# Joining the attention branches in two whole-width steps, with a new schedule table, in a one-core transformer block

## Chip, cores and metric

One NeuronCore of one Trainium2 chip runs the whole kernel in a single launch. The metric is the device time of one execution in microseconds (us); the program has the five engines TensorE (PE), VectorE (DVE), ScalarE (ACT), GpSimd (POOL) and SyncE (SP), each with its own instruction stream, and hand-placed semaphores between them.

## What is computed

One layer of a transformer over 1024 tokens of width 1024, in float32. The attention part has three families of four or eight heads of width 64: NSA (three branches, joined by a gate), sliding window with sinks (SWA) and stick-breaking (SB). The lines that matter for this change are those of the NSA family:

```python
def nsa_mixer(q, k_cmp, v_cmp, k_slc, v_slc, k_win, v_win, gate_logits, ...):
    ...
    o_cmp, o_slc = nsa_cmp_and_select(q, kc, vc, k_slc, v_slc, bias_tab)
    o_win = banded_attention(q[:, None], k_win[:, None], v_win[:, None], NSA_WINDOW, bias_tab)
    g = jax.nn.sigmoid(gate_logits.astype(jnp.float32)).reshape(b, s, 3, h).transpose(2, 0, 3, 1)[..., None]
    return g[0] * o_cmp + g[1] * o_slc + g[2] * o_win
...
    return jnp.concatenate([rms_norm(merge_heads(o_nsa), grp_g[:w_a]), rms_norm(merge_heads(o_swa), ...), rms_norm(merge_heads(o_sb), ...)], axis=-1)
...
        x = x + rms_norm(mix @ w_out[l], ln_attn_post[l])
        h = rms_norm(x, ln_ffn_pre[l])
        f = (jax.nn.silu(h @ ffn_w_gate[l]) * (h @ ffn_w_up[l])) @ ffn_w_down[l]
        x = x + rms_norm(f, ln_ffn_post[l])
```

## The kernel before

The time falls into three stages. Up to about 120 us the projections of the input are made. From there to about 505 us the attention runs. After that come the output projection and the feed-forward part, to the end at 1236 us.

The attention works in **jobs**. A job is one kind of attention (`sb`, `swa`, `win`, `cmp`, `slc`) for one tile of 128 query rows and four heads. There are 8 `sb`, 16 `swa` and 24 NSA jobs; the NSA ones come last, for each row tile in the order `win`, `cmp`, `slc`. Each job goes through the same steps. `query_hi`/`query_lo` split the queries (ACT L1269, DVE L1449), and four DMAs, `spread` on the SP queue (L812), place them for PE. `scores` on PE (L1070, L1078) multiplies queries and keys into one of four PSUM banks. `logits` on DVE (L1480) adds the bias and takes the running minimum `m_neg`; it frees the PSUM bank for the next `scores`. `softmax` on ACT (L1275) exponentiates. `turn` on PE (L1105) transposes the weights, `keep` copies them to SBUF (ACT L1305 or DVE L1510), and `weigh` on PE (L1125) multiplies them with the values into PSUM bank 7, the only bank for sums.

`combine` on DVE takes the sums out of bank 7. It first makes the four coefficients (L1533 or L1530, then a reciprocal, L1536). For `swa` and `win` one tensor_tensor of 128x256 multiplies all four heads with the coefficients, broadcast over the head width, into the tile `mix` (L1540). For `cmp` and `slc`, whose result is added to what is in `mix`, four scalar_tensor_tensor instructions of 128x64 do it, one for each head (L1546). The first `weigh` of the next job waits for the last instruction of the previous job's `combine`, as there is one bank of sums. After `slc`, `squares` on ACT (L1325), `mean_squares` on DVE (L1552), `root` on POOL (L894) and `norm_mix` on DVE (L1560) normalize `mix`, and PE transposes it (L1094).

The order of all this on each engine is fixed before the kernel is built, by the list scheduler `plan_attention`: every step has an engine, a cost, its needs and an age, and each engine takes the step that can begin first. Two tables written in the kernel bend it: `HELD` delays the moment from which a step may be taken, and `MOVED` shifts an age. Steps of low priority fill PE where nothing else is ready: `piece` (L988), the rest of the input projection, and `out_part` (L1136), the output projection of the first row tile, for which ACT and DVE cut the weights `o_w` (L1339, L1570). A wrong estimate in the planner costs no correctness; the engine then just waits at a semaphore.

```python
                if job.kind in ("swa", "win"):
                    ins = dve.tensor_tensor(mix[...].rearrange("p (h d) -> p h d", d=HD),
                                            sums[:, :, 0:HD], coef[:, a].unsqueeze(2).broadcast_to([P, 4, HD]), ALU.mult)
                else:
                    dve.wait_ge(combined, v)
                    for i in range(4):
                        ins = dve.scalar_tensor_tensor(out=dst, in0=sums[:, i, 0:HD], scalar=coef[:, a][:, i:i + 1], in1=dst,
                                                       op0=ALU.mult, op1=ALU.add)
                ins.then_inc(combined, 1)
```

At the end of the kernel the class `Finish` normalizes the output. POOL raises the mean squares to the power -1/2 there, with a tile of constants `mhalf` that POOL sets itself (`constants`).

Of the kernel before, what the change touches and what calls it, by code (L numbers as in the profile page):

```python
# [22 lines left out]
P = 128  # L23
# [4 lines left out]
HD = 64  # L28
# [211 lines left out]
def item_ends(n):  # L240
# [38 lines left out]
def plan_attention(lay):  # L279
# [55 lines left out]

    for j, job in enumerate(jobs):
# [63 lines left out]
        else:  # L400
            fresh = [("turn", lay.turn_at[job.family, n - 2])] if n >= 2 else [("turn", lay.turn_at["sb", NT - 1])] if job.kind == "swa" else []
            extra = [("sink_exp", lay.j_swa[j])] if job.kind == "swa" else []
            add(("combine", m), "dve", {"swa": 900, "win": 650}.get(job.kind, 1100), [last] + fresh + extra, age)
        if job.kind in ("sb", "slc") or job.strip == 4:
            i, width = NT * FAMILIES.index(job.family) + n, FAMILY_WIDTH[job.family]
            age = 10.0 * j + 20
            add(("squares", i), "act", act(width, 250), [("stick_combine", n) if job.kind == "sb" else ("combine", m)], age)
# [22 lines left out]
    for k in range(KT):  # L430
        add(("out_part", k), "pe", 6 * 226.5, [("out_lo", k), ("mix_lo", 0), ("logits", lay.c_sm[lay.NC] - 1)], 1e5)
# [62 lines left out]
def mixers(nc, core, x_rows, w_first, w_tiles, w_values, ln_pre, cmp, rel_bias, onehot, sinks, grp_g, w_out, ln_post, ln_ffn_pre, tables, keep):  # L494
# [15 lines left out]
    softmax_jobs = [j for j in range(lay.NJ) if jobs[j].kind != "sb"]  # L510
    NPHI = 8

    with ExitStack() as st:
# [96 lines left out]
        combined, stick_combined = sem("combined"), sem("stick_combined")  # L610
# [537 lines left out]
        def act_program(act, o):  # L1148
# [204 lines left out]
        def dve_program(dve, o):  # L1353
# [165 lines left out]
            def combine(v):  # L1519
# [19 lines left out]
                if job.kind in ("swa", "win"):  # L1539
                    ins = dve.tensor_tensor(mix[:, job.mix_at:job.mix_at + 4 * HD].rearrange("p (h d) -> p h d", d=HD),  # L1540
# [1045 lines left out]
class Finish:  # L2586
# [48 lines left out]
    def constants(self, pool):  # L2635
        pool.memset(self.mhalf[:], -0.5).then_inc(self.mhalf_set, 1)
# [230 lines left out]
```

## Time and profile before

| | before |
|---|---|
| median of 3 runs | 1236.33 us (1234.15 to 1237.01) |
| profiled execution, its time | 1238.16 us |
| span from first to last instruction in it | 1236.4 us |
| busy: PE / DVE / ACT / POOL | 1212.0 / 861.2 / 607.5 / 179.1 us |
| granted TensorE clock, mean | 0.995 of full speed |

The span is the time between the first and the last instruction of the profiled execution; 1.8 us of its own time lie around it. Busy times are unions of instruction records, and the records of neighbouring matmuls overlap, so a short stall of PE can be hidden inside them. PEld is the load of the stationary operand, which goes ahead of each matmul.

### The profile page before, as it was taken

The numbers are of one execution on the slowest core, as the hardware profiler recorded it, in microseconds if no ns is written. First come the engines' busy times: TensorE is split into PE (matmuls) and PEld (weight loads), VectorE is DVE, ScalarE is ACT, GpSimd is POOL, SyncE is SP. The second block draws the span as 40 slices with busy tenths as digits, with TensorE's granted clock in tenths as the row PEclk, the third lists the DMA queues.
The fourth block names the chain that finished last, engine by engine and source line by source line (L and its number), as shares of the span: only waits on it lengthen the run. The fifth ranks groups of instructions, "written<-read, shape, count | busy, mean of one in ns | idle before, by whom it ended". The sixth has DMA issues, their size and how long they took to land.

```text
span 1236.4 us, 18763 instructions
## 1 busy us (share of the span) xinstructions
PE 1212.0 (98%) x6592; PEld 1040.7 (84%) x6592; DVE 861.2 (70%) x1637; ACT 607.5 (49%) x1171; POOL 179.1 (14%) x153
## 2 busy tenths in 40 slices
PE   9999999999999999999999999999999999999996
PEld 7899788888989999888778888888888887788885
DVE  6322697968779765547966765756757668888888
ACT  5432687757777665443743333333333346444353
POOL 5230111111000000111001112211212120000114
PEclk9999999999999999999999999999999999999999
DMA  7303422136843000323213323133232356643443
GB/s 237 121 2 106 115 55 52 35 111 159 184 107 100 22 19 18 102 86 120 85 44 111 128 85 123 65 111 128 94 120 70 129 193 214 246 170 103 153 171 136
DMA packets 66882, 136.93 MB, mean 111 GB/s; under 512 B 8504, under 2 KB 27200, under 8 KB 66789
## 3 DMA queue, kind: packets, MB, share of 16 engines
q1 hardware_dynamic: 66788, 135.74, 34.6%
q8 instruction: 53, 0.87, 0.3%
q14 instruction: 41, 0.33, 0.1%
HBM read 90.33 MB, written 28.60 MB: 96 GB/s over the span
## 4 chain that ended last, share of the span: by engine, by line
PE 81%; DVE 7%; issue 4%; ACT 4%; DMA 2%; SPq 1%; DVEq 0%; POOL 0%; ACTq 0%; POOLq 0%
PE ps L2534 32%; PE ps L2564 12%; PE ps L1125 8%; PE ps L2478 6%; PE ps L969 4%; PE ps L1105 4%; PE ps L914 4%; PE ps L988 3%; PE ps L1070 2%; PE ps L1078 2%; PE ps L1003 1%; DVE ring L1496 1%; DMA m_qs<-m_qn 1%; SPq L812 1%; PE ps L1136 1%
## 5 line engine op out<-in xcount | busy, mean ns | idle before, releaser
L2534 PE MATMUL ps<-f_topH,f_W 128*128 128x512 f32 x704 | 221.0, 389 | 3.8 <-DVE f_W L2320 2.1
L2534 PEld LDWEIGHTS ps<-f_topH,f_W 128*128 128x128 f32 x704 | 132.1, 188 | 32.0 <-DVE f_W L2320 4.6
L2320 DVE TENSOR_TENSOR f_W<-f_scr,f_W 128x512 fp32r<-128x512 f32 (+1 forms) x128 | 89.8, 704 | 84.7 <-ACT f_W L2085 84.5
L2534 PE MATMUL ps<-f_topL,f_W 128*128 128x512 f32 x352 | 136.9, 389 | 0.0
L2564 PE MATMUL ps<-f_headH,f_W 128*128 128x512 f32 x408 | 127.9, 390 | 2.2 <-issue 1.5
L1125 PE MATMUL ps<-V,m_tw 128*128 128x66 f32 (+1 forms) x1056 | 127.8, 272 | 0.4 <-DVE m_mix_n L1546 0.3
L1125 PEld LDWEIGHTS ps<-V,m_tw 128*128 128x128 f32 x1056 | 125.2, 192 | 2.8 <-DVE m_mix_n L1546 1.6
L2534 PE MATMUL ps<-f_headH,f_W 128*128 128x512 f32 x352 | 114.7, 390 | 0.0
L2564 PEld LDWEIGHTS ps<-f_headH,f_W 128*128 128x128 f32 x408 | 76.6, 188 | 19.6 <-issue 2.8
L2085 ACT CAST f_W<-f_scr 128x512 fp32r<-128x512 f32 (+1 forms) x128 | 77.6, 610 | 24.6 <-PE ps L2564 15.0
L2320 DVE TENSOR_TENSOR f_W<-ring,f_W 128x512 fp32r<-128x512 f32 x60 | 59.5, 1005 | 33.5 <-ACT f_W L2085 33.3
L2564 PE MATMUL ps<-f_headL,f_W 128*128 128x512 f32 x204 | 79.4, 389 | 0.0
L2534 PEld LDWEIGHTS ps<-f_headH,f_W 128*128 128x128 f32 x352 | 66.1, 188 | 13.7
L2534 PEld LDWEIGHTS ps<-f_topL,f_W 128*128 128x128 f32 x352 | 66.1, 188 | 13.6
L1305 ACT COPY m_tw<-ps 128x512 f32<-128x512 f32 (+1 forms) x104 | 57.8, 570 | 34.4 <-PE ps L1125 22.5
L2534 PE MATMUL ps<-f_headL,f_W 128*128 128x512 f32 x176 | 68.5, 389 | 0.0
L2564 PE MATMUL ps<-f_b22H,f_W 128*128 128x512 f32 x208 | 65.2, 389 | 0.0
L2478 PE MATMUL ps<-o_w,o_mH 128*128 128x512 f32 x224 | 60.5, 392 | 0.0
L988 PE MATMUL ps<-m_hH,m_wH 128*128 128x512 f32 x144 | 59.5, 413 | 0.7 <-ACT QT L1206 0.7
L2534 PE MATMUL ps<-f_b22H,f_W 128*128 128x512 f32 x176 | 57.8, 389 | 0.0
L2353 DVE TENSOR_TENSOR QT<-ps,QT 128x512 f32<-128x512 f32 x68 | 46.6, 686 | 15.7 <-PE ps L2564 15.7
L988 PE MATMUL ps<-m_hH,m_wL 128*128 128x512 f32 x144 | 56.6, 393 | 0.0
(279 smaller groups left out, 2651.5 us busy)
## 6 DMA issues: line engine op xcount, KB each, us to landing
act_pairs<-QT SPq DMA_DIRECT2D x77, 256.0 KB, 4.1
m_qs<-m_qn SPq DMA_DIRECT2D x128, 128.0 KB, 2.5
ring<-in_ffn_w_up SPq DMA_DIRECT2D x22, 512.0 KB, 3.7
f_stage<-act_pairs SPq DMA_DIRECT2D x40, 256.0 KB, 3.6
ring<-in_ffn_w_gate SPq DMA_DIRECT2D x19, 512.0 KB, 4.6
f_scr<-act_pairs SPq DMA_DIRECT2D x37, 256.0 KB, 3.2
ring<-in_ffn_w_down SPq DMA_DIRECT2D x11, 512.0 KB, 5.5
f_pair_up<-in_ffn_w_down SPq DMA_DIRECT2D x11, 512.0 KB, 6.8
```

The lines of the kernel that those rows point to most:

```text
L914: return pe.matmul(ps[:, h, :], w[:, k % W_ITEMS, (h // 2) * P:(h // 2 + 1) * P], a[:, k, half_cols(h)], start=first, stop=last)
L969: ins = pe.matmul(ps[:, b + a, 0:VW_HALF], h[:, k, tok], wv[:, w, k, a * VW_HALF:(a + 1) * VW_HALF], start=(k == 0 and h is hH and w == 0) ...
L988: ins = pe.matmul(ps[:, bank, :], w[:, n % W_ITEMS, cols], a[:, k, hf * HALF:(hf + 1) * HALF], start=(k == 0 and w is wH and a is hH), sto ...
L1105: ins = pe.transpose(ps[:, bank, i * P:(i + 1) * P], rows, ident[:])
L1125: ins = pe.matmul(ps[:, SUMS, wide * i:wide * (i + 1)], tw[:, t % W_SLOTS, P * i:P * i + P], v, start=(kb == 0 and i == 0), stop=(kb == jo ...
L1305: act.copy(out, src).then_inc(kept_by["act"], 1)
L2085: act.copy(slot_part(s, 0), source(s)).then_inc(hi_done, 1)
L2320: dve.tensor_tensor(slot_part(s, 1), source(s), slot_part(s, 0).bitcast(F32), ALU.subtract).then_inc(lo_done, 1)
L2353: dve.tensor_tensor(part, product_, part, ALU.add).then_inc(y_added, 1)
L2478: ins = pe.matmul(ps[:, 2 * (t % 2) + hf, :], m[:, t % 2, k, :], w[k][:, a, hf * HALF:(hf + 1) * HALF], start=(k == 0 and m is mH and a == ...
L2534: ins = pe.matmul(ps[:, bank, :], whole[:, w, cols], halves[h][:, k0 + k, col:col + HALF], start=(begins and k == 0 and w == 0 and h == 0) ...
L2564: ins = pe.matmul(ps[:, bank, :], whole[:, w, k * P:(k + 1) * P], block(n)[h], start=(begins and k == 0 and w == 0 and h == 0), stop=(k == ...
```

## The change

`combine` of `cmp` and `slc` jobs now makes one tensor_tensor multiply of 128x256 from PSUM into a scratch tile `tmp` in SBUF and signals `combined`. A new step `mix_add` on DVE then adds `tmp` to `mix`, one tensor_tensor of 128x256 in SBUF. `tmp` belongs to the output projection, and its memory is in use by the input projection before, so the multiply waits for the last `piece`. It also waits for the previous `mix_add`. `squares` of the NSA family waits for the new semaphore `mix_added`. The planner knows the new step; its cost for `combine` is 800 for every kind, and that of `out_part` rises from 6 x 226.5 to 6 x 231. `HELD` and `MOVED` hold other entries throughout. The constants of `Finish` are gone: it reads a constant tile that was there already, broadcast where four columns are wanted, so one semaphore is used less.

```diff
 HELD = {
-    "combine": {36: 1000},
-    "cut_hi": {14: 1500, 16: 1500, 20: 500, 22: 2500},
-    "cut_lo": {15: 2500},
-    "half_hi": {11: 1500},
-    "half_keep": {16: 500},
-    "keep": {18: 500, 82: 500, 96: 500},
-    "logits": {78: 500, 88: 2500, 91: 500, 107: 500, 117: 1000, 179: 1000, 181: 2500},
-    "mean_squares": {21: 2500},
-    "scores": {48: 1000, 122: 1000, 134: 1000, 139: 2500, 141: 1000, 144: 1000, 170: 2500, 180: 2500, 183: 1000, 185: 1500},
-    "softmax": {157: 500},
-    "stick_combine": {2: 1000},
-    "stick_exp": {9: 2500, 18: 1500},
-    "stick_scan": {10: 500},
-    "stick_sub": {0: 500, 8: 1000, 18: 500},
-    "stick_weights": {19: 1000, 28: 2500},
-    "weigh": {12: 1000, 126: 1500},
+    "cut_hi": {22: 2500},
+    "keep": {6: 2500, 19: 2500, 24: 2500},
+    "logits": {65: 2500, 68: 1000, 119: 500, 149: 1000},
+    "mean_squares": {5: 2500},
+    "out_lo": {3: 500},
+    "root": {15: 2500},
+    "scores": {6: 1000, 23: 1500, 46: 1500, 161: 1000, 165: 2500, 186: 1500, 204: 2500},
+    "softmax": {51: 1000, 90: 1000},
+    "stick_combine": {4: 2500},
+    "stick_exp": {38: 1500},
+    "stick_sub": {25: 500},
+    "stick_weights": {25: 1500},
+    "turn": {6: 1500},
+    "weigh": {5: 2500, 9: 1000, 17: 500, 24: 2500, 27: 1500, 57: 500},
 }
 MOVED = {
-    "combine": {19: 60},
-    "logits": {93: 220},
-    "scores": {15: 400, 212: 180},
+    "half_keep": {11: -270},
+    "scores": {209: 545},
 }
...
-            add(("combine", m), "dve", {"swa": 900, "win": 650}.get(job.kind, 1100), [last] + fresh + extra, age)
+            two_step = job.kind in ("cmp", "slc")
+            added = [("mix_add", two_steps - 1)] if two_step and two_steps else []
+            add(("combine", m), "dve", 800, [last] + fresh + extra + added, age)
+            if two_step:
+                add(("mix_add", two_steps), "dve", dve(256), [("combine", m)], age + 0.5)
+                two_steps += 1
...
-        add(("out_part", k), "pe", 6 * 226.5, [("out_lo", k), ("mix_lo", 0), ("logits", lay.c_sm[lay.NC] - 1)], 1e5)
+        add(("out_part", k), "pe", 6 * 231, [("out_lo", k), ("mix_lo", 0), ("logits", lay.c_sm[lay.NC] - 1)], 1e5)
...
-                    act.wait_ge(combined, 2 * n + 2 if family == "swa" else 2 * NT + 3 * n + 3)
+                    if family == "swa":
+                        act.wait_ge(combined, 2 * n + 2)
+                    else:
+                        act.wait_ge(mix_added, 2 * n + 2)
...
                 if job.kind in ("swa", "win"):
-                    ins = dve.tensor_tensor(mix[:, job.mix_at:job.mix_at + 4 * HD].rearrange("p (h d) -> p h d", d=HD),
-                                            sums[:, :, 0:HD], coef[:, a].unsqueeze(2).broadcast_to([P, 4, HD]), ALU.mult)
+                    out = mix[:, job.mix_at:job.mix_at + 4 * HD]
                 else:
-                    dve.wait_ge(combined, v)
-                    for i in range(4):
-                        dst = mix[:, HD * i:HD * i + HD]
-                        ins = dve.scalar_tensor_tensor(out=dst, in0=sums[:, i, 0:HD], scalar=coef[:, a][:, i:i + 1], in1=dst,
-                                                       op0=ALU.mult, op1=ALU.add)
-                ins.then_inc(combined, 1)
+                    out = o["tmp"][:, 0:4 * HD]
+                    dve.wait_ge(piece_done, pieces(PIECES))
+                    if two_step_jobs.index(j):
+                        dve.wait_ge(mix_added, two_step_jobs.index(j))
+                dve.tensor_tensor(out.rearrange("p (h d) -> p h d", d=HD), sums[:, :, 0:HD],
+                                  coef[:, a].unsqueeze(2).broadcast_to([P, 4, HD]), ALU.mult).then_inc(combined, 1)
+
+            def mix_add(i):
+
+                j = two_step_jobs[i]
+                mix = mix_of("nsa", jobs[j].n)[:, 0:4 * HD]
+                dve.wait_ge(combined, j_sm[j] + 1)
+                if jobs[j].kind == "slc":
+                    dve.wait_ge(mix_added, i)
+                dve.tensor_tensor(mix, mix, o["tmp"][:, 0:4 * HD], ALU.add).then_inc(mix_added, 1)
...
-        fin.constants(pool)
...
-        pool.wait_ge(self.mhalf_set, 1)
         pool.wait_ge(self.ms_done, 1)
-        pool.tensor_tensor(self.rs[:, 0:M_PAIRS], self.ms[:, 0:M_PAIRS], self.mhalf[:], ALU.pow).then_inc(self.rs_done, 1)
+        pool.tensor_tensor(self.rs[:, 0:M_PAIRS], self.ms[:, 0:M_PAIRS], self.mhalf[:].broadcast_to([P, M_PAIRS]), ALU.pow).then_inc(self.rs_done, 1)
```

## Rows read from the trace of the kernel before

**Rows 1.** The page: busy us, share of the span, instructions of each engine.
```profile
PE 1212.0 (98%) x6592; PEld 1040.7 (84%) x6592; DVE 861.2 (70%) x1637; ACT 607.5 (49%) x1171; POOL 179.1 (14%) x153
```

**Rows 2.** Stretches: from:to, length, busy us by engine, clock, DMA share, GB/s.
```profile
325.00:364.00 39.00, 38.95 (x304) 36.73 (x303) 29.12 (x121) 26.67 (x72) 2.44 (x5) 1.00 0.43 102
364.00:400.00 36.00, 35.49 (x267) 31.75 (x264) 34.52 (x145) 29.83 (x66) 1.62 (x3) 1.00 0.39 113
400.00:440.00 40.00, 40.00 (x327) 38.60 (x326) 29.72 (x129) 25.93 (x48) 1.08 (x2) 1.00 0.16 39
440.00:485.00 45.00, 44.67 (x357) 41.83 (x356) 28.32 (x111) 28.24 (x49) 1.08 (x2) 1.00 0.04 11
```

**Rows 3.** Waits of PE's weight loads, 363 to 505 us: total, times, longest.
```profile
PEld ps L1070 <- DVE m_neg L1480: 2.6, 12, 0.4
PEld ps L1125 <- DVE m_mix_n L1546: 1.6, 5, 0.6
PEld ps L1094 <- ACT m_tw L1305: 0.5, 1, 0.5
PEld ps L1094 <- issue: 0.4, 2, 0.3
PEld ps L1125 <- DVE m_mix_n L1540: 0.4, 2, 0.2
PEld ps L1125 <- issue: 0.2, 1, 0.2
```

**Rows 4.** Waits of PE's weight loads, 100 to 363 us, the three longest.
```profile
PEld ps L1070 <- DMA m_qs<-m_qn: 3.1, 4, 1.7
PEld ps L1070 <- DVE m_rows_sb L1503: 1.7, 3, 1.0
PEld ps L1105 <- issue: 1.5, 3, 0.8
```

**Rows 5.** Line L1546: durations ns min/median/max, first and last start; who waited.
```profile
L1546 DVE SCALAR_TENSOR_TENSOR m_mix_n<-ps,m_coef,m_mix_n x64: 272/276/286, 367.3 to 498.2; 128x64 f32<-128x64 f32 x64
...
  PE ps L1125: 0.3, 1
```

**Rows 6.** DVE in order of time, around three `combine` steps: start, us.
```profile
366.85 0.16 DVE L1533 SCALAR_TENSOR_TENSOR m_coef<-ps,gate 128x4 f32<-128x4 f32 x1
367.04 0.18 DVE L1536 RECIPROCAL m_coef<-m_coef 128x4 f32<-128x4 f32 x1
367.26 0.86 DVE L1546 SCALAR_TENSOR_TENSOR m_mix_n<-ps,m_coef,m_mix_n 128x64 f32<-128x64 f32 x4
368.04 0.41 DVE L1480 CUSTOM_DVE_ANT_0 m_rows_slc<-ps,m_strip_full 128x256 f32<-128x256 f32 x1
...
374.43 0.42 DVE L1540 TENSOR_TENSOR m_mix_n<-ps,m_coef 128x256 f32<-128x256 f32 x1
374.77 0.55 DVE L1480 CUSTOM_DVE_ANT_0 m_rows_win<-ps,m_strip_full 128x384 f32<-128x384 f32 x1
...
377.14 0.42 DVE L1449 TENSOR_TENSOR m_qn<-QT,m_qn 128x256 fp32r<-128x256 f32 x1
377.47 0.18 DVE L1480 CUSTOM_DVE_ANT_0 m_rows_cmp<-ps,m_strip_full 128x23 f32<-128x23 f32 x1
```

**Rows 7.** All engines in order of time: two `weigh` steps behind a `combine`.
```profile
368.17 0.97 PEld L1125 LDWEIGHTS ps<-V,m_tw 128*128 128x128 f32 x8 [0.63 <-DVE m_mix_n L1546]
...
370.71 0.30 PEld L1125 LDWEIGHTS ps<-V,m_tw 128*128 128x128 f32 x2 [0.34 <-DVE m_mix_n L1546]
```

**Rows 8.** Line L1560, same columns as rows 5: a three-input operation of this width.
```profile
L1560 DVE SCALAR_TENSOR_TENSOR m_mix_n<-m_mix_n,m_rs,m_g_sb x8: 474/480/482, 373.2 to 501.3; 128x256 f32<-128x256 f32 x8
```

**Rows 9.** Line L988, same columns: the last product of `piece`.
```profile
L988 PE MATMUL ps<-m_hH,m_wL x144: 388/393/400, 122.6 to 361.8; 128*128 128x512 f32 x144
```

**Rows 10.** POOL in order of time, near the end of the kernel.
```profile
1211.53 1.02 POOL L2680 TENSOR_TENSOR e_rs<-e_ms,e_mhalf 128x4 f32<-128x4 f32 x1 [2.17 <-DVE e_ms L2663]
1212.52 3.54 POOL L2648 TENSOR_TENSOR QT<-QT,e_last_gain 128x512 f32<-128x512 f32 x2
```

**Rows 11.** PE in order of time, 499 to 504 us: around the last `turn`.
```profile
501.15 1.07 PE L1136 MATMUL ps<-o_w,o_mH 128*128 128x512 f32 x4
502.06 0.62 PE L1136 MATMUL ps<-o_w,o_mL 128*128 128x512 f32 x2
502.52 0.38 PE L1094 MATMUL ps<-ident,m_mix_n 128*128 128x128 f32 x2
502.65 1.17 PE L1136 MATMUL ps<-o_w,o_mH 128*128 128x512 f32 x4
```

More of the change, by code:

```diff
@@ L334, in plan_attention @@
     add(("strip", 4), "dma", 3000, [("norm_mix", NT - 1)], -100)
+    two_steps = 0
     for j, job in enumerate(jobs):
@@ L406, in plan_attention @@
             age = 10.0 * j + 20
-            add(("squares", i), "act", act(width, 250), [("stick_combine", n) if job.kind == "sb" else ("combine", m)], age)
+            add(("squares", i), "act", act(width, 250), [("stick_combine", n) if job.kind == "sb" else ("mix_add", two_steps - 1) if job.kind == "slc" else ("combine", m)], age)
             add(("mean_squares", i), "dve", 100, [("squares", i)], age)
@@ L510, in mixers @@
     softmax_jobs = [j for j in range(lay.NJ) if jobs[j].kind != "sb"]
+    two_step_jobs = [j for j in range(lay.NJ) if jobs[j].kind in ("cmp", "slc")]
     NPHI = 8
@@ L609, in mixers @@
         kept_by = {"act": sem("turn_kept_by_act"), "dve": sem("turn_kept_by_dve")}
-        combined, stick_combined = sem("combined"), sem("stick_combined")
+        combined, stick_combined, mix_added = sem("combined"), sem("stick_combined"), sem("mix_added")
         squares, ms_ready, rs_ready, normed = sem("squares"), sem("ms_ready"), sem("rs_ready"), sem("normed")
@@ L1579, in dve_program @@
                     "stick_scan": stick_scan, "stick_sub": stick_sub, "keep": keep_turn, "sink_arg": sink_arg_,
-                    "combine": combine, "mean_squares": mean_squares, "norm_mix": norm_mix}
+                    "combine": combine, "mix_add": mix_add, "mean_squares": mean_squares, "norm_mix": norm_mix}
             for what, arg in plan["dve"]:
@@ L2579, in pe_program @@
                 product(s)
-    o = {"w": w, "mH": mH, "mL": mL, "gpost": gpost, "gpre": gpre, "g_in": g_in, "wH_done": wH_done, "wL_done": wL_done,
+    o = {"w": w, "tmp": tmp, "mH": mH, "mL": mL, "gpost": gpost, "gpre": gpre, "g_in": g_in, "wH_done": wH_done, "wL_done": wL_done,
          "mH_done": mH_done, "mL_done": mL_done, "y_done": y_done}
@@ L2586, with __init__ @@
 class Finish:
-    def __init__(self, core, stack, x1, ln_post, out, y_part, xt, gain, gained_last, junk):
+    def __init__(self, core, stack, x1, ln_post, out, y_part, xt, gain, gained_last, junk, mhalf):
         sb = lambda n, s, d=F32: core.sb("e_" + n, s, d, stack)
@@ L2594, in __init__ @@
         self.y, self.xt, self.gain, self.gained_last, self.junk = y_part, xt, gain, gained_last, junk
-        self.ss, self.half, self.ms, self.rs, self.mhalf = sb("ss", [P, 2, NT]), sb("half", [P, NT]), sb("ms", [P, NT]), sb("rs", [P, NT]), sb("mhalf", [P, M_PAIRS])
+        self.ss, self.half, self.ms, self.rs = sb("ss", [P, 2, NT]), sb("half", [P, NT]), sb("ms", [P, NT]), sb("rs", [P, NT])
         self.x_in = [sem(f"x_in{t}") for t in range(4)]
-        self.g_in, self.mhalf_set = sem("g_in"), sem("mhalf_set")
+        self.g_in, self.mhalf = sem("g_in"), mhalf
         self.squares, self.gained, self.late_gained, self.late_ms = sem("squares"), sem("gained"), sem("late_gained"), sem("late_ms")
@@ L2633, in store_halves @@
             sp.dma_start(self.out[t * P:(t + 1) * P, cols], self.room(t)[:, cols]).then_inc(self.out_done, 16)
-    def constants(self, pool):
-        pool.memset(self.mhalf[:], -0.5).then_inc(self.mhalf_set, 1)
     def square(self, act, t, i):
@@ L2770, in build_layer @@
             fin = Finish(core, ffn, x1, ins["ln_ffn_post"], out, keep["QT"][:].rearrange("p k (h q) -> p (k h) q", h=2),
-                         (mem["xt_up"], mem["xt_sums"], mem["xt_spare"]), mem["last_gain"], mem["gained_last"], mem["last_junk"])
+                         (mem["xt_up"], mem["xt_sums"], mem["xt_spare"]), mem["last_gain"], mem["gained_last"], mem["last_junk"], mem["mhalf"])
             o, ffn_programs = out_and_ffn(nc, core, x, x1, ins["ffn_w_gate"], ins["ffn_w_up"], ins["ffn_w_down"], act_pairs, keep, mem, fin)
```

2 lines of the change are left out of this document (1 added, 1 removed).

## The prediction

> **What bounds the kernel now.** I read the page's busy shares first, then the stretches of the attention, then the waits of PE's weight loads, and last DVE's instructions in order of time. The page says that PE is busy for 1212.0 of 1236.4 us and DVE for 861.2 [rows 1]. So the kernel is bound by PE, and the change does not touch one PE instruction: it can only give back time in which PE stands still. The stretches show how little that is where the changed code runs. Between 364 and 485 us PE is busy for all but 0.51, 0.00 and 0.33 us [rows 2]. The busy time flatters PE, as records of neighbouring matmuls overlap, so I go by the weight loads, which stop as soon as a matmul is held back. From 363 to 505 us they waited 5.7 us in all (2.6 + 1.6 + 0.5 + 0.4 + 0.4 + 0.2), of which 1.6 us, in five waits, were for L1546, the four per-head instructions of `combine` [rows 3]. This is the ceiling of what the edit of `combine` can give by itself; the rest, 4.1 us, and the waits before 363 us are there for the table.
>
> **Part 1: the multiply out of PSUM.** In the old form the four instructions begin at 367.26 us and end 0.86 us later, at 368.12; the next job's first weight load starts at 368.17 [rows 6, 7]. A single multiply of 128x256 out of PSUM takes 0.42 us, which the `win` jobs show (L1540) [rows 6]. `combined` is now signalled behind it, so each of the 16 `weigh` steps behind a `cmp` or `slc` job is released 0.86 - 0.42 = 0.44 us earlier. Eleven of the 16 were not waited for and gain nothing. Of the five waits the one at 368.17 us was 0.63 us and keeps 0.19; the other four are 0.97 us together, the next one read being 0.34, and should go. That makes 1.6 - 0.2 = 1.4 us at most. The lower end is what the matmuls themselves show as idle, 0.3 us in one wait [rows 5]. I take 1.1 us, nearer to the upper end, because the matmul view hides stalls inside overlapping records while a few hundredths at each release remain whatever is done.
>
> **Part 2: the addition.** DVE must finish the multiply before it adds. The reciprocal ends at 367.22 us and its user starts at 367.26, so a dependent step follows about 0.04 us behind its source [rows 6]. The addition of 128x256 in SBUF is not in the trace; its nearest row is L1449, a subtraction of the same width from SBUF, 0.42 us long, behind which the next instruction starts 0.33 us after it did [rows 6]. The outer row is the three-input L1560 with 0.48 us [rows 8]. DVE is thus held for 0.42 + 0.04 + 0.33 = 0.79 us, where the four instructions hold it from 367.26 to 368.04, 0.78 us. By L1560 it would be 0.06 us more for each of 16, 1.0 us in all, on an engine with idle time in each stretch (1.5 us of 36 in the fullest one) [rows 2]. I count nothing, and up to 0.5 us of loss at the end of the range, for the case that half of it lands in the fullest stretch in front of `logits`.
>
> The per-head instructions are 276 ns each by median, yet four take 0.86 us and not 1.10, because each starts before the one ahead has ended [rows 5, 6]. The Trainium skill says otherwise in "VectorE: DVE Perf Modes", section "Rules for kernel authors": the pipeline drains behind every DVE operation, so one should cut the number of operations, not the semaphores. By that, two for four would save DVE about 1.10 - 0.84 = 0.26 us each time, some 4 us of DVE time over 16. The rows here disagree, and even if the rule held, it is DVE time and not PE time.
>
> **Part 3: the waits.** The multiply waits for the last `piece`. Its last product starts at 361.8 us, and the first multiply comes at 367.3 [rows 9, 5], so 5 us of cover; if a new order ran that piece later, the NSA transposes, which wait for the last half of the projection anyway, would be late first. The wait on the previous `mix_add` is behind it on the same engine and always met. Both stand in DVE's queue in front of `logits`, whose delay reaches PE as the twelve waits for L1480 [rows 3]; I cost them at nothing, at most 0.05 us each or 0.8 us of DVE's time in all, of which I let 0.2 us reach PE at the end of the range. `squares` waits for the addition: multiply, gap and addition end 0.42 + 0.04 + 0.42 = 0.88 us after the start, against 0.86. Even the last `squares`, in front of the last transpose, is covered: PE works through `out_part` around it without a gap [rows 11].
>
> **Part 4: the end.** One `memset` on POOL goes; POOL's root of four columns takes 1.02 us and is followed by gain products without a gap [rows 10]. Its operand is now broadcast. No wait of the end comes from either; nothing, within 0.1 us both ways.
>
> **Part 5: the new table.** This is the term that the trace can only bound. All of the attention's steps may change places, on five queues, the SP queue with its `spread` DMAs among them. What it can win at most is what the weight loads wait for: 4.1 us beside part 1 from 363 us on, and before that above all the 3.1, 1.7 and 1.5 us of [rows 4]. It can lose as well, since these waits were small in an order that fitted the old durations. The two planner costs that changed come nearer to the rows: old `combine` of `cmp` was planned at 1100, and it is 0.16 + 0.18 + 0.86 with gaps, 1.27 us, where the new one is (367.26 - 366.85) + 0.42 = 0.83 us against 800 planned. So the planner now sees `weigh` released about when it is. I take 1.0 us of gain, a quarter of the 4.1 us, in the NSA stretch and nothing before it, where no duration changes; the ends are 4 us of gain and 4 us of loss.
>
> **The sum** is -1.1 (part 1) - 1.0 (part 5) = -2.1 us. The profiled execution goes from 1238.16 to 1236.1 us. It was 1.8 us above the median of the runs, so on the median's footing the forecast is 1236.33 - 2.1 = 1234.2 us. A measurement of this kernel can tell a difference of about 0.2%, 2.5 us, from none: faster means under 1233.9 us, slower over 1238.8 us.
>
> **The rivals.** *First, the table finds more than I give it* (0.2). For it: the waits ahead of 363 us are twice those behind it, and three of them, 6.3 us, are at single places that a shift can cure [rows 4]. Against it: they are in steps whose durations stay, in an order that was already fitted to them. If two thirds of the 6.3 us go beside part 1: 1236.3 - 1.1 - 4.2 = 1231.0 us.
>
> *Second, the queries come late* (0.2), the case on the slower side. Each of the 32 groups of jobs starts with scores that wait for four `spread` DMAs, which stand in one SP queue behind `query_lo` on DVE. Four such waits cost 3.1 us, 0.78 each [rows 4]. An order that takes `query_lo` or a neighbour on SP later for one group costs PE that much when no `piece` is at hand, and from 362 us on none is [rows 9]. It decides from five groups on: 5 x 0.78 = 3.9 us, less 1.1, is 2.8 us of loss. With six it gives 1236.3 + 4.7 - 1.1 = 1239.9 us. For it: the table is new in every entry and delays seven `scores` and six `weigh`. Against it: from 325 to 364 us PE idled 0.05 us, so the group starts were well covered there [rows 2].
>
> *Third, the change does not do what it says to the end time* (0.1): the released `weigh` only brings PE sooner to the next wait, for L1480 or for ACT's `keep`, and the table neither wins nor loses. Then 1236.3 us.
>
> **How the numbers follow.** The forecast has 0.5, and as its middle lies 0.3 us above the bound of "faster" I give it 0.21 faster and 0.29 same. The first rival adds 0.2 to faster. The second adds 0.18 to slower and 0.02 to same. The third is same. That makes 0.41 faster, 0.41 same and 0.18 slower. The range goes from 1230.0, a little beyond the first rival, to 1239.5, which leaves out the far half of the second: with the bounds of parts 1 to 4 (0.4 us below the sum to 1.6 above) and most of part 5 inside, about 2 in 10 is left out.
>
> **What would show it.** L1546's 64 instructions are gone and 16 multiplies of about 0.42 us and 16 additions of about 0.42 us stand in their place, each addition 0.46 us behind its multiply; if the addition were 0.48 us or more, part 2 was too low. The weight loads' waits for `combine` in the NSA stretch fall from 1.6 us to about 0.3 us; if they stay, part 1 is wrong. The stretches from 364 to 485 us show PE idle under 0.84 us, and the attention ends about 2 us sooner, with the same shift at the end of the kernel; a shift in the attention that is not there at the end would speak against the bound by PE. More than four waits for the `m_qs` DMAs would be the second rival. No new wait for `piece` may stand in front of the first multiply.

## The result, and the profile after

| | before | after |
|---|---|---|
| median of 13 runs each, side by side | 1236.33 us (1233.91 to 1239.62) | 1240.0 us (1237.31 to 1242.31) |
| ratio | | 1.0026 [1.0016, 1.0036] |
| profiled execution, its time | 1238.16 us | 1241.11 us |
| span | 1236.4 us | 1239.3 us |

The changed kernel is slower by 0.26%, 3.2 us (2.0 to 4.4). Here and below the ratio is an estimate from all executions of both kernels, and not the quotient of the two medians, which are 3.7 us apart. The forecast was 1234.2 us with a range up to 1239.5: the sign is wrong, and the result lies above the range.

The page of the changed kernel, its span and its busy times, beside [rows 1]:

```profile
span 1239.3 us, 18737 instructions
PE 1212.8 (98%) x6592; PEld 1041.1 (84%) x6592; DVE 865.9 (70%) x1610; ACT 603.9 (49%) x1166; POOL 179.6 (14%) x152
```

PE has the same 6592 matmuls and 0.8 us more of them, but the span is 2.9 us longer: about 2.1 us are time in which PE stands still. Where it stands can be found with two marks that no order can move, the first product of the attention's planned part and the last product of its end. The rows are TensorE's, by tile `m_hid` and tile `o_mL`; the columns are duration min/median/max in ns, then first and last start. Before, then after:

```profile
L1038 PE MATMUL ps<-m_w,m_hid x4: 221/221/222, 128.0 to 128.2; 128*63 128x64 f32 x4
L1136 PE MATMUL ps<-o_w,o_mL x16: 387/389/395, 488.2 to 506.6; 128*128 128x512 f32 x16
```

```profile
L1042 PE MATMUL ps<-m_w,m_hid x4: 221/221/222, 126.4 to 126.6; 128*63 128x64 f32 x4
...
L1140 PE MATMUL ps<-o_w,o_mL x16: 387/389/397, 487.5 to 508.1; 128*128 128x512 f32 x16
```

From the last start of the one to the last start of the other are 506.6 - 128.2 = 378.4 us before and 508.1 - 126.6 = 381.5 us after: 3.1 us more. These 378.4 and 381.5 us are called the attention's time below. The rest of the span's difference cancels: the attention began 1.6 us earlier in this execution, and the part behind it took 1.5 us longer (731.25 us against 729.76). Neither follows the change: the first mark lies anywhere from 125.0 to 128.3 us in the executions with the old order and from 125.8 to 127.3 in those with the new one, and a second execution of the changed kernel took 729.7 us behind the attention, as before does. The code there is untouched but for POOL's constants.

The waits of PE's weight loads between those marks say what kind of time it is. The columns are total us, times, longest. Before:

```profile
PEld ps L1070 <- DMA m_qs<-m_qn: 3.1, 4, 1.7
PEld ps L1070 <- DVE m_neg L1480: 2.7, 13, 0.4
...
PEld ps L1125 <- DVE m_mix_n L1546: 1.6, 5, 0.6
PEld ps L1105 <- issue: 1.5, 3, 0.8
```

After:

```profile
PEld ps L1074 <- DVE m_neg L1487: 4.6, 17, 0.7
PEld ps L1109 <- issue: 3.1, 7, 1.2
PEld ps L1074 <- DMA m_qs<-m_qn: 2.7, 2, 2.0
...
PEld ps L1129 <- DVE o_tmp L1553: 0.5, 1, 0.5
```

All rows of this view together are 15.8 us before and 18.6 us after. The wait for `combine` fell, from 1.6 us in five waits to 0.5 in one. But the waits for the row minimum that `logits` writes (`m_neg`, L1487) rose from 2.7 to 4.6 us, and those put down to "issue" from 4.4 to 6.3 (all their rows together). The waits for `m_qs`, on which the second rival stood, did not rise, but two other rows did: the `scores` that wait for `m_rows_sb` from 1.7 to 2.1 us, and the transposes of `mix` that wait for a `keep` (L1094, now L1098) from 1.2 to 1.9.

The four stretches, beside [rows 2]:

```profile
325.00:364.00 39.00, 38.27 (x293) 35.87 (x294) 29.20 (x117) 24.99 (x66) 2.48 (x5) 1.00 0.46 107
364.00:400.00 36.00, 34.57 (x269) 32.26 (x269) 34.09 (x135) 30.08 (x69) 1.62 (x3) 1.00 0.40 116
400.00:440.00 40.00, 40.00 (x313) 36.96 (x313) 28.41 (x115) 25.42 (x47) 1.08 (x2) 1.00 0.13 32
440.00:485.00 45.00, 44.73 (x361) 42.24 (x359) 30.90 (x110) 28.02 (x49) 1.08 (x2) 1.00 0.04 9
```

PE stands still for 0.73, 1.43, 0.00 and 0.27 us. From 364 to 485 us that is 1.70 us where it was 0.84; the forecast asked for less than 0.84.

The new instructions themselves came out as foretold: multiply (L1553) and addition (L1563) in the changed kernel, columns as in [rows 5]:

```profile
L1553 DVE TENSOR_TENSOR o_tmp<-ps,m_coef x16: 423/424/425, 368.3 to 499.1; 128x256 f32<-128x256 f32 x16
```

```profile
L1563 DVE TENSOR_TENSOR m_mix_n<-m_mix_n,o_tmp x16: 412/417/426, 369.1 to 499.5; 128x256 f32<-128x256 f32 x16
```

So the parts are right and the whole is wrong. Either the edit of `combine` costs something elsewhere, or the new order does.

### The profile page after: what moved, and what is told of

It reads as the page before. It is cut to its first block, busy times and chain, and to the rows that moved or that the text cites. A ratio compares the mean times of both kernels' runs of the same rounds, so it can differ in the third digit from the quotient of the medians.

```text
span 1239.3 us, 18737 instructions
## 1 busy us (share of the span) xinstructions
PE 1212.8 (98%) x6592; PEld 1041.1 (84%) x6592; DVE 865.9 (70%) x1610; ACT 603.9 (49%) x1166; POOL 179.6 (14%) x152
## 4 chain that ended last, share of the span: by engine, by line
PE 81%; DVE 7%; issue 4%; ACT 4%; DMA 2%; SPq 1%; DVEq 0%; POOL 0%; ACTq 0%; POOLq 0%
PE ps L2548 32%; PE ps L2578 11%; PE ps L1129 8%; PE ps L2492 6%; PE ps L992 4%; PE ps L1109 4%; PE ps L973 4%; PE ps L1074 2%; PE ps L918 2%; PE ps L1082 2%; PE ps L1007 1%; DMA m_qs<-m_qn 1%; DVE ring L1503 1%; PE ps L1140 1%; DVE QT L2367 1%
```

## The experiments

**First: edit and order apart.** Theory A put the loss on the new order, theory B on the edit itself, theory C on something outside the attention. Theory B had a mechanism of its own: the addition stands in DVE's queue in front of `logits`. Four kernels, timed on one chip with 29 runs of before (median 1237.12 us).

*Edit alone.* The order, tables and costs of before; a `cmp` or `slc` job's `combine` is the multiply into `o_tmp` with the addition right behind it.

```diff
-                    dve.wait_ge(combined, v)
-                    for i in range(4):
...
+                    out = o["tmp"][:, 0:4 * HD]
...
+                if job.kind in ("cmp", "slc"):
...
+                    dve.tensor_tensor(mix[:, 0:4 * HD], mix[:, 0:4 * HD], o["tmp"][:, 0:4 * HD], ALU.add).then_inc(mix_added, 1)
```

> The order of every engine, the tables and the planner's costs are those of the kernel before; only combine of cmp and slc makes the one multiply and, right behind it, the one addition, and squares waits for the addition; the constants of Finish are gone as in the change. Theory A (the new order cost the time, the edit itself gave what was forecast): about 1.1 us faster than before, 1235.2 us, PE's weight loads wait about 0.5 us for combine in the NSA stretch instead of 1.6, and the waits for L1480's minimum stay at about 2.6 us. Theory B (the edit itself costs, because the addition stands in DVE's queue in front of logits): 2 to 4 us slower than before, and the waits for the minimum rise from 2.6 towards 4.6 us. Theory C (the difference lies in the feed-forward stage and its clock): same as before within 0.5 us, attention included.

*Order alone.* The order, tables and costs of after; `combine` does the four per-head instructions of before, `mix_add` does nothing.

```diff
             def mix_add(i):
...
-                dve.tensor_tensor(mix, mix, o["tmp"][:, 0:4 * HD], ALU.add).then_inc(mix_added, 1)
+                pass
```

> The order, tables and costs of the changed kernel, but combine of cmp and slc makes the four per-head instructions of before at the place of the multiply, and the step of the addition does nothing. Theory A: about 1 us slower than the changed kernel, 4 to 5 us slower than before, about 1241 us, with PE idle in the sliding-window stretch from 290 to 364 us as in the changed kernel (about 1.4 us by the busy view, where before had 0.5). Theory B: as before, 1236 to 1237 us. Theory C: as the changed kernel or as before by chance, with no difference where the attention ends.

*The two tables swapped.* After with the `HELD` and `MOVED` of before, and before with those of after (in both, only these two tables differ):

```diff
 HELD = {
-    "cut_hi": {22: 2500},
...
+    "combine": {36: 1000},
+    "cut_hi": {14: 1500, 16: 1500, 20: 500, 22: 2500},
...
```

> The changed kernel with the tables HELD and MOVED of before; the planner has the new step and the new costs, so that its order differs from both. Theory A: the table is only good for the plan that it was found with, so this is slower than before too, by 2 to 6 us; the edit's gain is hidden in it. Theory B: as the changed kernel, about 1240 us. If it comes out faster than before, the entries of the new table themselves are what costs.

> The kernel before with the tables HELD and MOVED of the changed kernel, old code and old planner costs. Theory A: 2 to 7 us slower than before, as a table fits only its own plan. If it is the same as before, then neither table matters much, and theory A falls with it.

| | median us | ratio to before | attention us in its trace |
|---|---|---|---|
| before | 1237.12 | | 378.4 |
| edit alone | 1236.98 | 1.0007 [0.9994, 1.0020] | 378.7 |
| order alone | 1240.41 | 1.0028 [1.0013, 1.0043] | 383.5 |
| after with the old table | 1239.29 | 1.0023 [1.0007, 1.0039] | 379.6 |
| before with the new table | 1247.11 | 1.0091 [1.0072, 1.0111] | 392.7 |

Edit alone is not to be told from before; order alone is slower than before by as much as the changed kernel is, and its attention is the longest of the first four rows. **The order costs the time.** Theory C falls with the attention of order alone, and of theory B the 2 to 4 us of loss: the interval of edit alone goes from 0.7 us faster to 2.5 us slower. That interval just leaves out the gain of 1.1 us that theory A gave the edit too, so only the half of theory A on the order is borne out. That order alone is slower than the changed kernel, as theory A had it, can't be told from the timed runs; its trace says so (383.5 us against 381.5). The idle time of PE from 290 to 364 us that it was to share with the changed kernel, 1.4 us, is 0.69 us in it.

The last row's trace has 6.8 us at half TensorE clock in its attention, so only its timed ratio is used: a table found for one set of durations makes the other code 0.9% slower, some 11 us and more than the 2 to 7 expected. The third row shows that the changed code is not better off with the old table either.

**Second: why the edit gains nothing in the old order.** The order of PE's work is that of before, so the two traces can be laid over each other wait by wait; around here edit alone runs some 3 us ahead of before, from a start of its attention 2.4 us earlier. Weight loads in order of time; the bracket is the idle time before the instruction and its releaser. Before (the two `weigh` waits ahead of these, 0.63 us at 368.17 and 0.34 at 370.71, are in [rows 7]):

```profile
372.81 0.19 PEld L1070 LDWEIGHTS ps<-m_KSa,m_qs 128*128 128x128 f32 x1 [0.24 <-DVE m_neg L1480]
...
377.27 0.86 PEld L1125 LDWEIGHTS ps<-V,m_tw 128*128 128x128 f32 x7 [0.19 <-DVE m_mix_n L1546]
```

Edit alone, from the same first `weigh` on:

```profile
364.97 0.97 PEld L1126 LDWEIGHTS ps<-V,m_tw 128*128 128x128 f32 x8 [0.19 <-DVE o_tmp L1550]
...
367.54 1.86 PEld L1126 LDWEIGHTS ps<-V,m_tw 128*128 128x128 f32 x16 [0.38 <-DVE o_tmp L1550]
370.05 0.19 PEld L1071 LDWEIGHTS ps<-m_KSa,m_qs 128*128 128x128 f32 x1 [0.65 <-DVE m_neg L1484]
...
377.39 0.19 PEld L1071 LDWEIGHTS ps<-m_KSa,m_qs 128*128 128x128 f32 x1 [0.56 <-DVE m_neg L1484]
```

The first `weigh` waits 0.19 us instead of 0.63, as the forecast had it. The second waits no shorter, 0.38 for 0.34: its multiply starts 2.57 us behind the first one (2.54 before) and releases it 0.4 us earlier, but PE, which is now 0.43 us early, is there earlier by as much, so nothing is added to the gain. Then the `scores` that waited 0.24 us waits 0.65: the whole gain of 0.4 us is handed back there. Further on a `weigh` wait of 0.19 us is gone (that of 377.27), and a `scores` behind it waits 0.56 us where before shows 0.13: 0.2 us more is given back than was gained. DVE's queue around the first `combine`, in order of time, shows why:

```profile
364.49 0.42 DVE L1550 TENSOR_TENSOR o_tmp<-ps,m_coef 128x256 f32<-128x256 f32 x1
364.95 0.42 DVE L1557 TENSOR_TENSOR m_mix_n<-m_mix_n,o_tmp 128x256 f32<-128x256 f32 x1
365.30 0.41 DVE L1484 CUSTOM_DVE_ANT_0 m_rows_slc<-ps,m_strip_full 128x256 f32<-128x256 f32 x1
```

The multiply is done after 0.42 us, but the `logits` behind the pair start 0.81 us after it did (365.30 - 364.49), where before they started 0.78 us after [rows 6]. The pair releases `weigh` early and nothing else. The next `logits`, and with them the `m_neg` that the next `scores` waits for, come when they did. Over 363 to 505 us the waits of edit alone are, beside [rows 3]:

```profile
PEld ps L1071 <- DVE m_neg L1484: 4.0, 14, 0.6
PEld ps L1126 <- DVE m_mix_n L1550: 0.6, 2, 0.4
PEld ps L1126 <- DVE o_tmp L1550: 0.6, 2, 0.4
```

The waits for any `combine` fell from 2.0 to 1.2 us, those for the minimum rose from 2.6 to 4.0, as theory B had it. Weight load by weight load, edit alone is 2.76 us ahead of before in front of the first of these waits and 2.15 us ahead at 482 us, so over the NSA part the edit by itself loses 0.6 us.

**Third: is it DVE's load there?** Theory D said that DVE is the bound from 364 to 400 us (34.3 of 36 us busy) and that with less work there the gain would come through; theory E that the load has no part. Six 1.22 us steps (`out_lo` 0 to 3, `mix_lo` 0 and 1) were moved out of 367 to 393 us to idle places behind 422 us, once on top of edit alone, once on top of before. In both, the loads from DRAM for the last four of the eight tiles of `o_w`, which wait for such steps, go to the end of the SP queue as well. Before and after were run a second time with them, to see how well a trace repeats.

```diff
+LATER = {
+    ('out_lo', 0): ('logits', 148),
+    ('mix_lo', 0): ('keep', 125),
...
+    for step, behind in LATER.items():
+        plan["dve"].remove(step)
+        plan["dve"].insert(plan["dve"].index(behind) + 1, step)
+    for k in range(RING, KT):
+        plan["dma"].remove(("out", k))
+        plan["dma"].append(("out", k))
```

> The kernel of e1 (edit alone, old order), but six steps of DVE that nothing needs before 480 us, out_lo 0 to 3 and mix_lo 0 and 1 of 1.22 us each, stand where DVE was idle between 422 and 470 us instead of between 367 and 393 us; the weight loads from DRAM that wait for them are issued last on the SP queue. Theory D (in the old order the five releases of weigh gained 1.1 us and the next scores gave it back, because DVE is the bound from 364 to 400 us): the waits for L1480's minimum after 363 us fall from 4.0 us to about 2 us, and the attention gets 1.5 to 2.5 us shorter than in e1 and in before; time about 1235 us. Rival E (the waits for the minimum come from the fixed distance between a score and the freeing of its PSUM bank, not from DVE's load): no change against e1, within 0.3 us.

> The kernel before (four per-head instructions, its order) with the same six steps moved later. Theory D: DVE is relieved here as well, but the five waits for combine, 1.6 us, stay; the attention is 0.5 to 1.2 us shorter than in before and about 1 us longer than in e5. Rival E: as before, and e5 and e6 differ as e1 and before do, by 0.2 us.

> The changed kernel once more, for a second profile. Theory A: the stretch from the last m_hid product to the last out_part is 381.5 us again, within 0.7 us, and longer than in before by about 3 us; the half-clock stretches lie elsewhere. If it is under 380 us, the loss in the attention was one execution's.

> The kernel before once more, for a second profile. Theory A: the same stretch is 378.4 us again, within 0.7 us.

The edit with the cuts moved ran in 1236.65 us, ratio 1.0002 [0.9991, 1.0013]; before with them moved in 1235.03, 0.9987 [0.9975, 0.9998]. Their attentions are 378.6 and 377.5 us. The stretch and the wait of the former:

```profile
364.00:400.00 36.00, 35.18 (x272) 32.47 (x272) 28.93 (x127) 29.29 (x64) 1.62 (x3) 1.00 0.21 52
```

```profile
PEld ps L1087 <- DVE m_neg L1500: 4.0, 15, 0.7
```

DVE lost 5.3 us of work in the stretch, and the wait for the minimum stayed at 4.0 us, with the attention of edit alone (378.7). So theory D falls, and edit alone and edit with the cuts moved agree within 0.1 us, as theory E had it. Before with the cuts moved is 1.1 us shorter than the edit with them moved, which neither theory had. What is left is that the wait is for what stands directly ahead in DVE's queue, which the next experiment tries. The second executions took 1237.71 us for after and 1237.09 for before, with an attention of 380.2 and 377.9 us. That of before was as expected; that of after is 1.3 us shorter than the first, twice the 0.7 us allowed, but still 2.3 us longer than before's. So a single attention is good to about 1.3 us, and the loss is 2.3 to 3.1 us.

**Fourth: the addition's place.** Theory F: it is the addition ahead of `logits` that eats the release, so it must go behind them; theory G: something else does. The addition of a `cmp` job is a step of its own, put behind the next two `logits`, `keep` or `query_lo`; once on edit alone, once with the cuts moved as well.

```diff
+PAST = {"cmp": 2, "slc": 0}
...
+        at = plan["dve"].index(("combine", lay.j_sm[j])) + 1
+        for _ in range(PAST[jobs[j].kind]):
+            at += plan["dve"][at][0] in ("logits", "keep", "query_lo")
+        plan["dve"].insert(at, ("mix_add", i))
```

> The kernel of e1 (edit in the old order), but after each cmp job the addition is a step of its own on DVE and stands behind the next two steps of kind logits, keep or query_lo; after slc jobs it stays right behind the multiply. Theory F (e1 gained nothing because DVE is free for the next logits only when the addition is done, 0.02 us later than before, so that the released weigh runs into the wait for the minimum): here the next logits starts 0.75 us after the coefficients and not 1.20 us, the waits for the minimum after 363 us fall from 4.0 us towards 2.6 us or less, and the attention is about 1 us shorter than e1's 378.7 us. Rival G (the minimum is late for another reason, such as logits waiting for its scores): waits of 4.0 us and 378.7 us as in e1.

> The kernel of e5 (edit in the old order, six cuts moved later) with the addition of the cmp jobs behind the next two steps as in e9. Theory F: about 1 us less attention than e5's 378.6 us, 377.6 us, near e6's 377.5; time about 1235.5 us, the fastest with the edit. Rival G: as e5.

DVE with the addition moved, around the same `combine` and the wait for the minimum, 363 to 505 us:

```profile
364.54 0.42 DVE L1558 TENSOR_TENSOR o_tmp<-ps,m_coef 128x256 f32<-128x256 f32 x1
364.88 0.41 DVE L1492 CUSTOM_DVE_ANT_0 m_rows_slc<-ps,m_strip_full 128x256 f32<-128x256 f32 x1
...
365.56 0.42 DVE L1568 TENSOR_TENSOR m_mix_n<-m_mix_n,o_tmp 128x256 f32<-128x256 f32 x1
```

```profile
PEld ps L1079 <- DVE m_neg L1492: 3.0, 10, 0.8
```

The next `logits` starts 0.34 us behind the multiply instead of 0.81, and the waits for the minimum fall from 4.0 to 3.0 us (14 waits to 10), not to 2.6. The whole attention did not get the expected 1 us shorter (378.6 us with the addition moved, 377.4 with the cuts moved too, which was expected). To see the effect, take the part from the last `weigh` of the `swa` jobs to the last `out_part`, which is the stretch the edit acts on and which repeats far better than the whole (147.08 us in both executions of before; the other kernels have one trace each, save after):

```
                                  as it is     cuts moved
before                             147.08        146.76
edit alone                         147.69        146.90
edit, addition behind logits       147.02        146.14
```

The edit by itself costs 0.6 us there. With the addition moved it is level with before, and with the cuts moved as well it gains 0.6 us over before with the same cuts. So theory F holds: moving the addition is worth 0.7 us. Moving the cuts is worth 0.3 us to before and 0.8 us to the edit, by another way than the wait that theory D named; whether that is DVE or the loads moved with them was not tried. In the whole time none of it can be seen: 1237.10 us, 1.0011 [0.9997, 1.0025], and 1236.75 us, 0.9998 [0.9987, 1.0009].

**Fifth: how good is the plan?** After with both tables empty.

```diff
-HELD = {
...
+HELD = {}
+MOVED = {}
```

> The changed kernel with empty tables HELD and MOVED. The planner's own span for this order is 11.4 us longer than for the changed kernel's (385.5 against 374.1). If the planner's differences held on the chip, the attention would be 11 us longer than the changed kernel's 380.2 to 381.5 us. Theory A (a searched table wins on paper by taking away slack, and part of that is not there on the chip): it is longer by clearly less, 6 to 10 us.

It took 1258.98 us, 1.0182 [1.0158, 1.0205], some 22 us more than before. The attention of its trace is 15 to 16 us longer than after's, where 6 to 10 was expected: a miss. Part of that is the clock: its attention holds two short stretches, at 212 and 383 us, together 6.8 us, in which the granted clock is half, which costs up to 3.4 us; PE had waited 2.6 and 2.0 us shortly ahead of them. What is left, 11.6 to 12.9 us, is about the 11.4 us that the planner gives. The planner's own end of the attention, next to the chip's (us; the chip's is the time between the two marks above; two executions where two stand; * with 6.8 us at half clock):

```
                            planner     chip
before                       374.1      378.4, 377.9
after                        374.1      381.5, 380.2
after, table of before       378.1      379.6
before, table of after       380.6      392.7*
after, no table              385.5      396.5*
```

By the planner after is as good as before, and 4.0 us better than with the old table; on the chip it is 2 to 3 us worse than before and 0.6 to 1.9 us worse than with the old table. The planner is right about the two orders that it finds much worse. **Among the first three its error is 1.5 us, 3.8 to 4.3 us and 6.1 to 7.4 us, so between after and either of the others it differs by more than these orders do in its own count.**

**Sixth: what the edit is worth in the new order.** The plan of after, but each addition moved back right behind its multiply (in after, 14 of the 16 have another step between, mostly a `keep` or a `logits`).

```diff
+    for i, step in enumerate(combines):
+        plan["dve"].remove(("mix_add", i))
+        plan["dve"].insert(plan["dve"].index(step) + 1, ("mix_add", i))
```

> The changed kernel, its order kept, but each of the 16 additions stands right behind its multiply on DVE; in the changed kernel 14 of them have a keep, a logits or another step in between. In the stretch from the last weigh of the sliding-window jobs to the last out_part the changed kernel took 150.9 us in both profiles and the same order with four per-head instructions 153.3 us. Theory F (the multiply's early release and the early start of DVE's next step each give part of the 2.4 us, and the second part exists only because the addition is a step of its own): 151.5 to 152.5 us here, 0.6 to 1.6 us longer than in the changed kernel. Rival H (all of it comes from the release of weigh): 150.9 us as in the changed kernel.

It ran in 1239.41 us, 1.0024 [1.0015, 1.0034]. Waits of PE's weight loads, 363 to 505 us, first in order alone and then here (to 507 us); after has 4.6 us in 17 waits for the minimum and 0.5 for `o_tmp`:

```profile
PEld ps L1074 <- DVE m_neg L1487: 4.8, 17, 0.7
PEld ps L1129 <- DVE m_mix_n L1553: 2.1, 6, 0.6
```

```profile
PEld ps L1078 <- DVE m_neg L1491: 5.3, 19, 0.7
...
PEld ps L1133 <- DVE o_tmp L1557: 0.5, 1, 0.5
```

The part behind the last `swa` `weigh` is 153.27 us for order alone, 151.68 here, and 150.85 and 150.94 for the two executions of after. In the new order the early release is thus worth 1.6 us and the free place of the addition another 0.8, as theory F had it (with 150.9 us here all of it would have come from the release): the edit gives 2.4 us back of what the order costs. The same release with the addition right behind it, which costs 0.6 us in the old order, gains 1.6 us in this one.

**Where the order loses.** Attention by stage, from the traces (in us, worked out from the starts of the stages' last PE steps; in brackets what the planner has for the two orders):

```
                      to the last swa weigh      from there to the last out_part
before, twice         231.4  230.8  (228.0)      147.1  147.1  (146.2)
after, twice          230.7  229.2  (224.5)      150.9  150.9  (149.7)
order alone           230.2                      153.3
```

The new plan moves 3.5 us of PE's work across that boundary, to behind it (16 of its matmuls, 1134 there instead of 1118). The part ahead should have shrunk by as much and shrank by only about 1.4 us (mean of the seven executions in the old order 231.2, of the four in the new 229.8), so about 2 us are lost there. Behind it order alone is 6.2 us longer, 2.7 us more than was moved, and the edit gives nearly all of that back: the changed kernel is 3.8 us longer there. The waits that came with the order stand at fixed places. PE in order of time, three executions in the new order (after, its second execution, order alone):

```profile
155.05 0.47 PE L1074 MATMUL ps<-m_KSb,m_qs 128*128 128x512 f32 x1 [0.54 <-DVE m_rows_sb L1510]
...
368.54 0.85 PE L1109 MATMUL ps<-ident,m_rows_win 128*128 128x128 f32 x6 [0.99 <-ACT m_rows_win L1279]
```

```profile
154.46 0.47 PE L1074 MATMUL ps<-m_KSb,m_qs 128*128 128x512 f32 x1 [0.54 <-DVE m_rows_sb L1510]
...
366.57 1.06 PE L1109 MATMUL ps<-ident,m_rows_win 128*128 128x128 f32 x8 [1.00 <-ACT m_rows_win L1279]
```

```profile
153.87 0.48 PE L1074 MATMUL ps<-m_KSb,m_qs 128*128 128x512 f32 x1 [0.55 <-DVE m_rows_sb L1510]
...
367.35 1.06 PE L1109 MATMUL ps<-ident,m_rows_win 128*128 128x128 f32 x8 [1.00 <-ACT m_rows_win L1279]
```

A `scores` in the `sb` stage waits 0.54, 0.54 and 0.55 us, and a `turn` waits 0.99, 1.00 and 1.00 for ACT's `win` softmax, a wait that PE doesn't have at all before. They belong to the order, not to chance, and no single one makes up the loss. Which entry of the table makes each was not tried.

## Why the prediction was wrong

*The bound.* Right: PE's busy time moved by 0.8 us, and the loss is idle time of PE in the attention, 2.3 to 3.1 us of the 3.2 us in time.

*Part 1, the multiply out of PSUM (-1.1 us).* Right in size, wrong in the step from the five waits to the end. In the old order the `weigh` starts of edit alone gain 0.43, 0.22, 0.25 and 0.23 us at four places, 1.1 us together, which is the term. All of it and 0.6 us more is handed back at the next waits, mostly those of `scores`. The five waits were added up as if PE ran on freely behind each, while [rows 3] already had twelve waits for L1480's minimum between them. This is the mechanism of the third rival, which had 0.1, and it is what happened to the edit by itself. In the new order, for which the forecast was made, the early release was worth 1.6 us, so this term did not make the sum too low; that it came near there is luck, as [rows 3] is of the other order.

*Part 2, the addition (0).* The sizes held: 417 ns by median against 0.42 estimated, started 0.46 us behind the multiply in edit alone, and the next instruction followed 0.81 us after the multiply, against 0.79 counted. "I count nothing" was right of DVE's time, but an addition that costs nothing there still keeps `logits` where it was, and so helps to undo part 1 in the old order. In the new order most additions stand elsewhere, and that was worth 0.8 us, which the sum did not have. The Trainium skill's rule that was weighed there, to keep the count of operations low ("VectorE: DVE Perf Modes", section "Rules for kernel authors"), did not give what the prediction worked out by it, some 4 us less of DVE's time: DVE is busy for 861.4 us in edit alone and 861.2 in before. This doesn't speak against the rule itself, as the prediction had it, for the work is not the same: the two instructions go over 512 columns, the four over 256.

*Part 3, the waits (0).* Right. No wait for `piece` stands in front of the first multiply: it starts at 368.3 us. The last transpose is not late.

*Part 4, the end (0).* Right: one POOL instruction less (153 to 152), and the time behind the attention shows nothing that follows the change. From the last `out_part` on it scatters by 2.4 us over all fourteen traces (728.8 to 731.2), of that by 0.6 and 1.5 us between the two executions of before and of after.

*Part 5, the table (-1.0 us).* **This is the step that failed.** The order by itself costs 3.5 us (ratio 1.0028, 1.6 to 5.3 us) in time and 5.0 us in its one trace (good to about 1.3 us), against a gain of 1.0 foretold and an end of 4 us of loss. With the 1.6 and 0.8 us that the edit gives back in this order, the traces add up to +5.0 - 1.6 - 0.8 = 2.6 us, where the forecast had -1.1 - 1.0, and 2.3 to 3.1 us were measured. "A quarter of the 4.1 us" had no row behind it. It rested on the planner seeing `combine` better than before, which is true, while the planner's error over the whole attention, which its planned end against the trace of before would have shown (374.1 against 378.4 us), is as large as all that a table could win there. The loss ends of all terms together reach 1234.2 + 1.6 + 5.0 = 1240.8 us, which holds the result; the range stopped at 1239.5, short of them.

*The second rival (slower, by late queries).* The sign, and by luck the price (1239.9 us), but not the mechanism: the waits for `m_qs` are 2.7 us after and 3.1 before, with none from 290 us on in the changed kernel. What came instead is many places of 0.3 to 1.0 us on `logits`, `softmax` and `turn`.

What stays open is which table entries cause the fixed waits, and whether the shortest NSA part (146.14 us, addition behind `logits` and cuts moved) is also the shortest kernel. The timed runs can't tell it from before. The only version that came out ahead of before is before itself with the six steps and the four loads moved: 0.9987 [0.9975, 0.9998], and that interval all but touches 1.

## What to carry to other kernels

A wait that is removed is worth only what the next waits on the same engine leave of it: here less than nothing in one order and 1.6 us in another. Where a second release comes soon behind the first, ask what stands between the two in the producer's queue, and put the work that nobody waits for (here the addition) behind what somebody does wait for. An order found by a planner is a change of its own, to be measured apart from the edit it comes with. As long as the planner misses the chip by more than two of its orders differ, its preference for one of them says nothing.

## What the runs showed of the hardware

Not expected: the whole time scatters by some 10 us (1233.3 to 1243.1 us over 29 runs of before, with a mean granted clock of 0.998 and 0.991 in these two), while the part behind the last `swa` `weigh` was 147.08 us in both executions of before and 150.85 and 150.94 in those of after. Part of the scatter is short stretches in which TensorE runs at its lower level, 1.2 instead of 2.4 GHz, and which differ between executions of one kernel: at 53.4 and 101.2 us in the first of before, at 8.0 and 55.8 in the second, at 54.2 and 1068.0 in the first of after, at 99.1 and 617.9 in its second. They are not at chance places either. Seven of the fourteen traces have one that begins between 52 and 56 us. In all fourteen traces PE waits for 2.12 or 2.13 us once between 612 and 634 us; in seven of them the clock falls 0.5 to 1.5 us behind that wait, and in the other seven it does not. The one at 1068 us, in the stretch 1060 to 1070 us of after:

```profile
1060.00:1070.00 10.00, 8.16 (x33) 6.34 (x32) 6.89 (x13) 3.32 (x7) 0.00 (x0) 0.90 0.85 336
```

The mean granted clock is 0.90 there, and 1.00 in the same stretch of before. PE had waited 1.8 us just ahead of it. So one trace against one trace is not a measure of a few us at the end of the kernel. A stage between two marks, taken twice, is: the part behind the last `swa` `weigh` repeated within 0.1 us, the attention as a whole within 0.6 and 1.3.
